# Leaving TensorE's unread identity products out of the three expert mixtures of a three-layer transformer kernel

## The reference, cut to what matters

```python
h = x * (1 + sc2) + sh2
# mixture: per token one of 4 groups, in it the best 2 of 8 experts (32 experts in all)
pg = softmax(xt @ w_group + b_group);  g_prob, g_idx = top_k(pg, 1)
e_prob, e_local = top_k(softmax(le_of_group), 2);  gates = g_prob * e_prob / sum(e_prob)
# the 2048 pairs of token and expert are sorted by expert, in blocks of 128 rows
y_block = (silu(xb @ w_gate[e]) * (xb @ w_up[e])) @ w_down[e]
out[token] += gate * y
x = layer_norm(alpha * x + (1 + g2) * out)
```

## Time and profile before

| | us |
|---|---|
| three runs, median | 3713.72 |
| their lowest and highest | 3711.33, 3714.51 |
| the profiled execution | 3712.36 |
| its span in the profile | 3710.5 |
| TensorE busy in the span | 3417.3 (92%) |
| VectorE busy | 1618.9 (44%) |

### The profile page before, as it was taken

How to read it: one execution, slowest core, us unless ns; L and a number is a source line. 1 busy time by engine, 2 the same in 40 slices (tenths; PEclk the granted TensorE clock), 3 DMA queues, 4 the chain that set the end, 5 groups by cost and what they waited for, 6 DMA issues and landing times. The chain is left out here.

```text
span 3710.5 us, 51510 instructions
## 1 busy us (share of the span) xinstructions
PE 3417.3 (92%) x20876; PEld 1742.5 (47%) x20876; DVE 1618.9 (44%) x2553; ACT 815.8 (22%) x1815; POOL 364.4 (10%) x355
## 2 busy tenths in 40 slices
PE   7999999899999899999997999998899978998996
PEld 3444565433333344777754333333555658553332
DVE  3760886510111475777756111113332865462114
ACT  0000660100000122555501000000333551111112
POOL 1000300210000000000001200000000920003110
PEclk9999999999999999999998999999999989999998
DMA  9980211599999621000023999997323301319996
GB/s 383 360 318 0 92 67 71 223 409 426 424 423 422 243 91 52 31 1 1 1 92 160 390 426 425 427 421 305 118 81 108 123 1 61 119 65 361 419 418 265
DMA packets 146837, 818.41 MB, mean 221 GB/s; under 512 B 30019, under 2 KB 35779, under 8 KB 100518
## 3 DMA queue, kind: packets, MB, share of 16 engines
q1 hardware_dynamic: 117622, 737.20, 49.9%
q0 software_dynamic: 25808, 68.88, 4.8%
q10 hardware_dynamic: 3168, 8.96, 0.6%
HBM read 752.52 MB, written 82.55 MB: 225 GB/s over the span
## 5 line engine op out<-in xcount | busy, mean ns | idle before, releaser
L2289 PE MATMUL m_yp<-m_w,m_hidT 128*32 128x512 f32 (+2 forms) x2248 | 381.2, 600 | 12.0 <-issue 6.1
L2266 PE MATMUL m_up<-m_w,m_xT 128*32 128x512 f32 (+2 forms) x1792 | 304.2, 605 | 25.9 <-DMA m_w<-in_moe_w_up 25.9
L2266 PE MATMUL m_gp<-m_w,m_xT 128*32 128x512 f32 (+2 forms) x1792 | 297.4, 594 | 8.4 <-DVE m_xT L1910 4.5
L2047 DVE TENSOR_TENSOR m_hid<-m_sg,m_up 128x512 f32<-128x512 f32 x42 | 28.9, 687 | 572.9 <-PE m_up L2266 572.9
L2042 DVE TENSOR_TENSOR m_yt<-m_yp,keep_flat 128x512 f32<-128x512 f32 x128 | 82.4, 685 | 403.8 <-PE m_yp L2289 394.6
L419 PE MATMUL front_acc<-front_hT,front_wt 128*128 128x512 f32 x512 | 224.5, 599 | 5.8 <-DMA front_wt<-in_na_w_qkv 5.8
L2289 PEld LDWEIGHTS m_yp<-m_w,m_hidT 128*32 128x32 f32 (+2 forms) x2248 | 123.0, 124 | 222.7 <-issue 217.7
L2266 PEld LDWEIGHTS m_up<-m_w,m_xT 128*32 128x32 f32 (+2 forms) x1792 | 104.8, 126 | 219.8 <-issue 219.8
L2347 ACT ACTIVATE m_sg<-m_gp 128x512 f32<-128x512 f32 (+1 forms) x64 | 33.5, 524 | 768.7 <-PE m_gp L2266 549.6
L1202 PE MATMUL n_acc<-n_wt,n_hT 128*128 128x512 f32 (+2 forms) x512 | 192.2, 532 | 2.8 <-DMA n_wt<-in_w_in 2.1
L2266 PEld LDWEIGHTS m_gp<-m_w,m_xT 128*32 128x32 f32 (+2 forms) x1792 | 97.4, 123 | 202.3 <-issue 197.1
(11 more groups left out here) (502 smaller groups left out, 4984.2 us busy)
## 6 DMA issues: line engine op xcount, KB each, us to landing
m_w<-in_moe_w_gate SPq DMA_DIRECT2D x64, 2048.0 KB, 28.7
m_w<-in_moe_w_up SPq DMA_DIRECT2D x64, 2048.0 KB, 27.8
m_w<-in_moe_w_down SPq DMA_DIRECT2D x64, 2048.0 KB, 29.8
v<-in_ada_w SPq DMA_DIRECT2D x40, 1024.0 KB, 12.6
m_w<-in_moe_w_gate SPq DMA_DIRECT2D x32, 1024.0 KB, 28.2
m_w<-in_moe_w_up SPq DMA_DIRECT2D x32, 1024.0 KB, 29.6
m_w<-in_moe_w_down SPq DMA_DIRECT2D x32, 1024.0 KB, 31.0
v<-in_w_mod SPq DMA_DIRECT2D x24, 1024.0 KB, 11.0
```

The costliest lines, as they stand in the source:

```text
L2266: last = pe.matmul(acc[part, 0:F], xT[:, j, k, part], w[:, place_of[m_, r][0], k * F:(k + 1) * F], start=k == 0, stop=k == KC - 1)
L2289: last = pe.matmul(yp[e][part, :], hidT[:, k, part], w[:, place_of["d", r][0], k * D + e * 512:k * D + (e + 1) * 512], start=k == 0, stop= ...
```

## The change

The three calls in `mixture` go. That is 13 products in each mixture and 39 in the program. The calls in all other stages stay, and no wait, no transfer and no other instruction is changed.

```diff
@@ -2290,10 +2290,8 @@
-                keep_clock(pe, turn[0], ident, 4)
                 count()
                 plan()
-                keep_clock(pe, turn[0], ident, 5)
                 list_rows()
                 pe.sem_inc(so_dn, 1)
                 spills = spilled(pe)
```

## The result

The changed kernel runs in 3719.07 us (median of 20 runs, 3713.13 to 3722.91) and the kernel before, also in 20 runs, in 3711.70 us (3708.02 to 3718.73). The ratio is 1.0017, with an interval of 1.001 to 1.0023. By it the change costs about 6.3 us, by the medians 7.4. So the size needs an explanation. The profiled execution of the changed kernel took 3722.91 us (span 3721.1), the longest of its 20, against 3712.36 before; of the 10.6 us between the two, part is that one run's own.

What follows compares the result with a forecast made beforehand. Weight transfers were taken to bound the mixtures. TensorE's delays of 4.3 us (m0), 0.9 (m1) and 4.9 (m2) vanish in waits except 1 us in m2: 3713.4, plus 1.4 for the median, 3714.7 us; range 3709 to 3722.

Steps and rivals of the forecast that it cites:

- Transfers set the mixtures: Each mixture ends by its first load's date plus its transfers, while TensorE's lateness is below its later waits for weights.
- The list: List of rows in each mixture: later by 2.1 us in m0 and 2.7 in m1 and m2.
- Block 0: First block's gate products: start 2 to 3 us later in m0 and m2, a little earlier (1.3 us) in m1.
- m2: Last mixture: token and weight waits swallow the delay, or up to 2.3 us is left; 1 us taken.
- slow starts: TensorE after idling, at list_rows and block 0: slower clock costs 1.6 to 2.4 us each; 2.4 and 2.2 taken.
- The date of `m_pl`: Cast of m_pl, on which the first load hangs: moves by 0, bounds 0 and 0.5 us in each mixture.
- The waits: TensorE's waits for weights shrink by about 4 us in m0, 1 in m1 and 2.7 in m2.
- the cover: Lateness a mixture can swallow, read from later waits: 16.8 us in m0, 12.1 in m1, 5.1 plus 3.5 in m2.
- the rest of the program at 0: Stages outside the mixtures: no term in the sum, so the 1 us for m2 stood for the whole program.
- first rival: Mixtures: loads' landing moves with TensorE, so the late starts add up to 10.1 us, 3723.8 us; chance 0.14.
- The second: Rival: clock stays low for all of the list and much of block 0, +3.8 us, 3717.5; chance 0.10.
- The third: Rival: products are on the path, so removal is faster, 3708.2 us, or 3696.2 without clock loss; chance 0.06.

Runs made afterwards that it cites:

- late runs: Kernel before with 16 products instead of 4 just ahead of block 0: in m0 and m1, plus 40 tiny ones in m1, 1.0018; in m2 alone, 0.9997.
- late first load: Kernel before with the five products between plan and list_rows moved ahead of plan in all three mixtures; 1.0022, 3718.99 us.
- second profile: The changed kernel run again unaltered, on one chip with three other kernels; 1.0016 (1.0007 to 1.0025), scan 53.20 us. Also called the repeat.
- tiny products: Kernel before with its 39 products replaced by as many of 32 x 32 elements, keeping the number of instructions; 0.9995 (0.9986 to 1.0004).

## Why the prediction was right or wrong

The measured time lies inside the range, and what the prediction says of the mixtures holds in the main. What moved the time lies outside them.

**Transfers set the mixtures: right.** The three together are 0.7 us longer. The late runs in m0 and m2 show that 9 us of lateness vanish, and the late first load that its date does count. The stages behind don't start within 1 us of their old times, as the prediction said: `n1` is 1.5 us later, `n3` 1.7 and `n5` 10.2. Of the 10.2 the scan has 5.2. The way there was partly off. The list was later by 1.8, 2.6 and 1.8 us (`m_pu`, line 2019, behind the list's start) for a forecast of 2.1, 2.7 and 2.7. Block 0 started 1.9 later in m0 (2.1 forecast) and 1.0 earlier in m1 (1.3).

**m2: wrong in detail, right in the end.** Block 0 started 5.1 us later instead of 2.7 (43.98 behind the list's start, 38.86 before): the copy on VectorE (line 1910) came behind 8.17 us that only its loop explains, where 5.14 were taken from m0. TensorE in m2, after:

```profile
3376.65 1.96 PE L2238 MATMUL m_turn<-keep_ident,m_x 128*128 128x128 f32 x8 [14.49 <-issue]
3382.71 8.52 PE L2258 MATMUL m_gp<-m_w,m_xT 128*128 128x512 f32 x16 [4.10 <-issue]
```

Of the 0 to 2.3 us that the sum left there the runs show at most a part: with the products left out m2 is 0.6 and 1.1 us longer in two profiles, and left out of m2 alone they give 0.9996 (0.9987 to 1.0005), an interval that ends at 1.9 us.

**The slow starts: somewhat too dear.** Block 0's gate products take 8.5 us in each mixture (8.6 to 9.0 in the second profile); I had 9.3, so 1.4 us a start in place of 2.2. `list_rows` takes 5.45 to 6.25 us (5 to 6.1 forecast), a cost of 1.8 to 2.6 against the 2.4 taken. The date of `m_pl` didn't move at all.

**The waits: right in m0 and m2, wrong in m1.** They shrank by 4.5 us in m0 (about 4 forecast) and by all 3.5 in m2 (2.7), but in m1 those for the up matrices grew by 1.5 (1 less forecast). The late runs say more: m1, with 12.1 us of these waits, lost 7.6 of 14.1 us and still waited 11.3, and m2, with 8.6 us of waits, swallowed 9.5. So the sum of the later waits, which the prediction took for the depth of the cover, isn't it.

**The term that failed: the rest of the program at 0.** The sum values nothing outside the mixtures, because no other instruction is changed. Its place in the instruction stream is. The scan of `gdn` went from 48.24 to 53.47 us, 5.2 us for a measured difference of 6.3. That the forecast's range held this is luck: its 1 us was meant for m2, and its upper end for half of the first rival. Seven traces with a shift of 0 or 64 products give 47.5 to 48.4 us, four with -26 or +38 give 53.1 to 53.5, whatever was done to the work in the mixtures. No row ahead of the prediction showed it, because the idle times called "issue" inside `gdn` weren't looked at. They were there in the trace before, but it couldn't say what another position would cost.

**The rivals.** The first (lateness rides through, +10.1) has its mechanism, as m1 with 14 us of it shows, but with the change the end of block 0's gate products is later by only 3.3 us in m0 (1.9 + 1.4), 0.4 in m1 and 6.5 in m2, below the 9 that were swallowed in m0 and m2. The +6.3 measured looks like a part of this rival and has nothing to do with it. The second (+3.8) had a list later by 5.8 us, and it is 2.6 at most; its 0.5 us for each first load is 0. The third (products on the path) forecast a gain, and the time has grown. The tiny products bear it out: 0.9995 with the work gone.

**What stays open.** Of the 10.6 us between the two profiled executions 5.2 are in the scan and 0.7 in the mixtures. The rest is spread over other stages, 1.9 of it in `n3`. `n3` takes 293.54 us after and 293.51 in the kernel with m0 and m1 left out, and 292.84 in the repeat, against 291.65 before and 291.7 to 292.7 in the five experiments that keep its position up to there; whether that is the same effect was not tried. No long stall of `n3` ends behind a packet as those of the scan do. Why a packet comes late in `gdn` wasn't tried either. The rate was about 400 GB/s there in both kernels, but it isn't the packet's own transfer that is slow: the four packets from 3138 to 3160 us before take 0.93 to 1.26 us, and the median of all 172 is 1.07. What is late is its start: the packet of 3145.61 starts 0.3 us behind the start of the stall that it ends.

## What to carry to other kernels

Products that only keep TensorE busy were worth nothing here, where transfers set the time and their queue wasn't short. So first find the date of the first load, and measure the depth of the cover by making the engine late, since the sum of its waits didn't give it. Only then think of the clock. When instructions are added or left out, the change moves all later code of that engine relative to the packets in which it is fetched; test it against a kernel that keeps their number with tiny ones, or a loss or gain elsewhere will be put down to the edit. In a stage of very short products look for idle times with no releaser, count the records up to each, and look for an instruction packet landing just ahead of its end.

## What was not expected of the hardware

- TensorE's instructions arrive in packets of 16.4 KB. In `gdn`, where 913 records pass in 48 us, it idles 1.2 to 3.2 us at steps of about 125 records, and not at every one, and goes on 1.3 to 1.6 us behind the landing of a packet (36 stalls in 14 traces). The same work takes 47.5 to 53.5 us, depending on its position.
- The idle time is the smaller part of it in the changed kernel's first profile: 6.4 us of long stalls against 5.0 before. The larger is the clock behind them, at 0.83 instead of 0.93 over the stretch (3.9 us more of busy time). In the second profile, at 0.86, they are 7.5 us of stalls and 2.3 us more of busy time.
- m2 swallowed 9.5 us of lateness of TensorE and m0 8.9, with nothing of it in the time of the stage; m1 lost 7.6 of 14.1 us.
